# A gated convolution and neighbourhood-attention block: first norm weights as a row, conv tiles read three at a time, four reorderings in the queues

## What is computed

```python
h = rmsnorm(x, norm_g); proj = h @ w_in            # 1024 -> 9 x 1024
a_val, a_glu, z_a, q, k, v, z_b, g_logits = split(proj)
u   = a_val * sigmoid(a_glu)
c   = depthwise_conv31(u) + dw_b
y_a = (silu(layernorm(c, ln_g, ln_b)) * silu(z_a)) @ w_pw_a
attn = neighbourhood_attention(q, k, v, rpb)       # 16 heads, windows of 8 rows x 16 columns
y_b = (attn * silu(z_b)) @ w_o_b
merged = sigmoid(g_a) * y_a + sigmoid(g_b) * y_b   # gates from g_logits + b_gate
y = rmsnorm(x + merged @ w_out, final_g)
```

## Time and profile before

| | |
|---|---|
| median of 3 runs | 1765.33 us |
| the profiled execution, its own time | 1764.42 us |
| its span (first to last instruction) | 1762.5 us |
| PE, DVE, ACT, POOL busy | 1733.1, 1172.5, 468.3, 207.0 us |
| share of PE in the chain that ended last | 92% |
| mean granted TensorE clock | 0.996 |

### The profile page before, as it was taken

How to read it: one execution, slowest core, us unless ns; L and a number is a source line. 1 busy time by engine, 2 the same in 40 slices (tenths; PEclk the granted TensorE clock), 3 DMA queues, 4 the chain that set the end, 5 groups by cost and what they waited for, 6 DMA issues and landing times.

```text
span 1762.5 us, 24610 instructions
## 1 busy us (share of the span) xinstructions
PE 1733.1 (98%) x8652; PEld 1411.5 (80%) x8652; DVE 1172.5 (67%) x1765; ACT 468.3 (27%) x925; POOL 207.0 (12%) x250
## 2 busy tenths in 40 slices
PE   7999999999999999999999999999999899999998
PEld 6888877888888888888887888888777778887886
DVE  4439255897688589579768948957975677335332
ACT  5421123123122122222312212222224234102222
POOL 1120011011011011101101101110200063000001
PEclk9999999999999999999999999999999899999999
DMA  7151335545436525534543562553567565543223
GB/s 289 56 106 48 99 99 143 159 122 160 123 90 170 159 61 156 149 95 133 155 126 85 169 166 54 145 168 90 141 200 291 175 192 179 191 133 105 73 84 132
DMA packets 293893, 240.97 MB, mean 137 GB/s; under 512 B 117222, under 2 KB 248310, under 8 KB 293658
## 3 DMA queue, kind: packets, MB, share of 16 engines
q1 hardware_dynamic: 241482, 145.69, 30.3%
q10 hardware_dynamic: 48432, 79.97, 13.3%
q0 software_dynamic: 3872, 13.75, 3.0%
HBM read 155.10 MB, written 84.23 MB: 136 GB/s over the span
## 4 chain that ended last, share of the span: by engine, by line
PE 92%; DVE 3%; DMA 3%; ACT 1%; issue 1%; ACTq 0%; SPq 0%; DVEq 0%
PE pg L1436 69%; PE pg L1454 15%; PE pO L1546 4%; PE pS L1529 3%; DVE work L1325 2%; DMA qk<-gb_d 1%; DMA work<-tb_d 1%; DVE xs L1065 1%; DMA work<-p_d 1%; ACT xs L828 0%; DMA raw<-in_w_in 0%; DVE ws L1057 0%; PE pS L1470 0%; DVE work L1346 0%; PE pO L1470 0%
## 5 line engine op out<-in xcount | busy, mean ns | idle before, releaser
L1436 PE MATMUL pg<-xs,ws 128*128 128x512 f32 x5688 | 1317.7, 392 | 8.9 <-DVE work L1346 6.6
L1436 PEld LDWEIGHTS pg<-xs,ws 128*128 128x128 f32 x5688 | 1064.7, 188 | 244.7 <-issue 15.2
L1141 DVE SCALAR_TENSOR_TENSOR work<-work 128x1551 f32<-128x1551 f32 x240 | 438.4, 1827 | 4.6
L1454 PE MATMUL pg<-ws,xs 128*128 128x512 f32 x1008 | 238.7, 393 | 3.3 <-DVE ws L1057 2.2
L1454 PEld LDWEIGHTS pg<-ws,xs 128*128 128x128 f32 x1008 | 189.8, 189 | 44.0 <-DVE ws L1057 4.1
L646 POOL TENSOR_TENSOR work<-work 128x384 f32<-128x384 bf16 (+1 forms) x72 | 62.7, 870 | 984.2 <-DVE small L1213 973.7
L1213 DVE CUSTOM_DVE_ANT_0 work<-pS,work 128x384 f32<-128x384 f32 (+1 forms) x192 | 88.4, 511 | 114.9 <-PE pS L1529 114.8
L916 ACT ACTIVATE work<-work,small 128x384 f32<-128x384 f32 (+1 forms) x192 | 109.2, 570 | 158.4 <-DVE small L1213 158.4
L1057 DVE TENSOR_TENSOR ws<-raw,ws 128x1024 fp32r<-128x1024 f32 x89 | 109.7, 1234 | 48.5 <-ACT ws L697 48.4
L697 ACT ACTIVATE ws<-raw 128x1024 fp32r<-128x1024 f32 x89 | 93.5, 1053 | 119.4 <-PE pg L1436 98.7
L1225 DVE STREAM_TRANSPOSE work<-work 128x384 f32<-128x384 f32 (+1 forms) x192 | 102.6, 534 | 6.6
(11 more groups left out here) (98 smaller groups left out, 928.4 us busy)
## 6 DMA issues: line engine op xcount, KB each, us to landing
raw<-in_w_in SPq DMA_DIRECT2D x70, 512.0 KB, 4.5
p_d<-work SPq DMA_DIRECT2D x256, 96.0 KB, 2.2
work<-p_d ACTq DMA_DIRECT2D x64, 384.0 KB, 4.5
work<-v_d SPq DMA_DIRECT2D x128, 96.0 KB, 2.7
p_d<-work SPq DMA_DIRECT2D x128, 64.0 KB, 1.9
work<-p_d ACTq DMA_DIRECT2D x32, 256.0 KB, 4.4
v_d<-work ACTq DMA_DIRECT2D x24, 256.0 KB, 2.0
za_d<-work ACTq DMA_DIRECT2D x24, 256.0 KB, 2.1
```

What stands on the lines that cost most here:

```text
L1141: nc.vector.scalar_tensor_tensor(cv[:, 0:CLEN], u[:, k:k + CLEN], cur[:, k:k + 1], cv[:, 0:CLEN], ALU.mult, ALU.add).then_inc(tap_ok, 1)
L1436: last = nc.tensor.matmul(pg[b][:], wt(s, wpart)[:, k * P:(k + 1) * P], xs[:, k, xpart, chunk(n)], start=(k == 0 and wpart == 1), stop=(k ...
L1454: last = nc.tensor.matmul(pg[b][:], xs[:, k, xpart, t * P:(t + 1) * P], wt(s0 + k // 2, wpart)[:, chunk(k % 2)], start=(k == 0 and xpart = ...
```

## The change

There are five parts. (1) `norm_g` is also loaded as one row of 4 KB, by a transfer issued from ACT's queue; PE multiplies a row of 128 ones with it (two matmuls with a contraction of 1) so that it stands in two PSUM banks on all partitions, and four transposes of the identity run ahead of them. `normalise(0)` reads these banks, in two halves, each with its own count, and PE transposes half by half. The 512 KB load to all partitions stays for the other token tiles and moves behind weight pieces 0 and 1 and token tile 1. (2) In the last unit the two early `tb_d` loads move behind the stores of blocks 10 and 11. (3) In SP's loop of phases 1 and 2 the gate tile is loaded ahead of the weight piece. (4) From the fourth on, conv tile k is loaded once the mean has been taken off tile k-3. (5) On DVE, piece S_OUT+3 is split after two of the eight subtractions of `refill_lo(3, 1)` and `gate(47)`; the other six follow it.

```diff
--- before.py
+++ after.py
@@ -213,6 +213,8 @@
         ngb = work[:, 9 * D:10 * D]
         raw2 = work[:, 11520:11520 + 2 * D].rearrange("p (s d) -> p s d", s=2)
         msk32 = work[:, 11520:11520 + MASKLEN]
+        grow = work[0:1, 15680:15680 + D]
+        onerow = work[0:1, 16704:16704 + P]
         prow = work[:, 14656:14656 + D]
         table = work[:, 0:RROWS * RCOLS]
 
@@ -300,7 +302,7 @@
         x_hi, x_lo = sem("x_hi"), sem("x_lo")
         w_ld = [sem(f"w_ld{i}") for i in range(2)]
         w_ld2 = [sem(f"w_ld2{i}") for i in range(2)]
-        ng_in = sem("ng_in")
+        ng_in, gr_in, ng_ps = sem("ng_in"), sem("gr_in"), sem("ng_ps")
         w_hi, w_lo = sem("w_hi"), sem("w_lo")
         w_used = sem("w_used")
         g_done = sem("g_done")
@@ -428,10 +430,10 @@
                 sp.dma_start(xt[:, t % 8, :], tok_rows(x_prompt, x_sample, t)).then_inc(x_in[t % 8], 16)
 
             load_x(0)
-            sp.dma_start(ngb, norm_g[0:1, :].to_broadcast([P, D])).then_inc(ng_in, 16)
             for s in range(2):
                 piece_s(s, w_rows(w0, C_V * P, s))
             load_x(1)
+            sp.dma_start(ngb, norm_g[0:1, :].to_broadcast([P, D])).then_inc(ng_in, 16)
             for s in range(2, 4):
                 piece_s(s, w_rows(w0, C_V * P, s))
             for t in range(2, 8):
@@ -524,11 +526,11 @@
                         piece(s, w_tile(w0, i * P + ahead[n] * P), 8 * i + (s - 1))
                     elif last and n == 4:
                         piece_y(S_YB)
-                    if last and n == 5:
-                        load_tb_early()
                     if n < BLOCKS // 2:
                         store_probs(i, 2 * n)
                         store_probs(i, 2 * n + 1)
+                    if last and n == 5:
+                        load_tb_early()
                     if n == 4 and not last:
                         load_rel(i + 1, 18 * i + 18)
                     if n == len(ahead) - 2 and n >= 6 or n == 5 and len(ahead) == 6:
@@ -568,13 +570,13 @@
                 sp.wait_ge(st_out[n], 128 + 48 * PAIRS)
             for e in range(2 * 24):
                 ct, n = (e % 24) // NCH, e % NCH
-                if n == 0:
-                    piece_y(S_YB + e // NCH + 3)
                 if e >= 3:
 
                     b, _, out = grs(G_YB + e - 3)
                     sp.wait_ge(g_out[b], out)
                     load_gate(e)
+                if n == 0:
+                    piece_y(S_YB + e // NCH + 3)
                 if e == 24:
 
                     sp.wait_ge(ta_ok, 3 * KT)
@@ -613,7 +615,8 @@
         def _(pool):
             nc.gpsimd.memset(ident[:], 0.0).then_inc(const_ok, 1)
             nc.gpsimd.memset(half, -0.5).then_inc(const_ok, 1)
-            pool.wait_ge(const_ok, 2)
+            nc.gpsimd.memset(onerow, 1.0).then_inc(const_ok, 1)
+            pool.wait_ge(const_ok, 3)
             nc.gpsimd.affine_select(out=ident[:], in_=ident[:], compare_op=ALU.not_equal, fill=1.0, base=0,
                                     pattern=[[-1, P]], channel_multiplier=1).then_inc(const_ok, 1)
             for t in range(NT):
@@ -657,6 +660,8 @@
             for k in range(KT):
 
                 pool.wait_ge(x_lo, 5 * KT + k + 1 if k < KT - 2 else 6 * KT)
+                if k >= 3:
+                    pool.wait_ge(dev, k - 2)
                 pool.dma_start(cs[:, k, :], c_d[k]).then_inc(c_in[k], 16)
 
             pool.wait_ge(var_ok, 1)
@@ -750,6 +755,7 @@
                 act.dma_start(v_d[t * P:(t + 1) * P, chunk(c)], stage[:, g % 3, :]).then_inc(st_out[g % 3], 16)
 
 
+            act.dma_start(grow, norm_g[0:1, :]).then_inc(gr_in, 16)
             square(0)
             split_s(0)
             h_hi(0, 0)
@@ -1074,9 +1080,15 @@
 
             def normalise(t):
 
+                dve.wait_ge(rstd_ok, t + 1)
                 if t == 0:
+                    for hf in range(2):
+                        dve.wait_ge(ng_ps, hf + 1)
+                        x = xt[:, 0, chunk(hf)]
+                        nc.vector.scalar_tensor_tensor(x, x, rstd[:, 0:1], pS[hf][:], ALU.mult, ALU.mult).then_inc(xn_ok, 1)
+                    return
+                if t == 1:
                     dve.wait_ge(ng_in, 16)
-                dve.wait_ge(rstd_ok, t + 1)
                 x = xt[:, t % 8, :]
                 nc.vector.scalar_tensor_tensor(x, x, rstd[:, t:t + 1], ngb, ALU.mult, ALU.mult).then_inc(xn_ok, 1)
 
@@ -1365,10 +1377,12 @@
                     if tile == KT - 1 and n >= 1:
                         if n == 1 and phase == 3:
                             split_s(S_OUT + 2)
-                        refill_lo(phase, n - 1, lambda k: cs[:, k, chunk(n - 1)], 0.5)
+                        ks = range(2) if n == 2 and phase == 3 else range(KT)
+                        refill_lo(phase, n - 1, lambda k: cs[:, k, chunk(n - 1)], 0.5, ks)
                 gate(e0 + 23)
                 if phase == 3:
                     split_s(S_OUT + 3)
+                    refill_lo(phase, 1, lambda k: cs[:, k, chunk(1)], 0.5, range(2, KT))
                 else:
                     refill_lo(phase, 2, lambda k: cs[:, k, chunk(2)], 0.5)
 
@@ -1461,8 +1475,8 @@
 
             def h_t(t):
 
-                pe.wait_ge(xn_ok, t + 1)
                 for hf in range(2):
+                    pe.wait_ge(xn_ok, t + 2 if t else hf + 1)
                     if 2 * t + hf >= 4:
 
                         pe.wait_ge(x_lo, 2 * t + hf - 3)
@@ -1479,7 +1493,12 @@
                                                ident[0:NPAR, 0:NPAR])
                 last.then_inc(par_ps, 1)
 
-            pe.wait_ge(const_ok, 3)
+            pe.wait_ge(const_ok, 4)
+            for k in range(4):
+                nc.tensor.transpose(pg[1][:, k * P:(k + 1) * P], ident[:], ident[:])
+            pe.wait_ge(gr_in, 16)
+            for hf in range(2):
+                nc.tensor.matmul(pS[hf][:], onerow, grow[:, chunk(hf)], start=True, stop=True).then_inc(ng_ps, 1)
             h_t(0)
             for t in range(NT):
                 token_group(t, 0, t, 0, True, t + 1 if t + 1 < NT else None)
```

## The result

The changed kernel takes 1749.22 us in the median of 4 runs (1746.58 to 1750.26), the kernel before 1765.14 beside it; the ratio is 0.9912, 95% interval 0.9900 to 0.9924. On a second chip it was 1749.17 against 1764.15, ratio 0.9918 (0.9902 to 0.9935). That is 15 to 16 us where 11.5 were forecast, and the time lies 2 us under the range. The profiled execution has a span of 1744.8 us against 1762.5.

What follows compares the result with a forecast made beforehand. PE was taken as the bound, busy 1733.1 of 1762.5 us, leaving about 30 us to win. Gains of 0.7 + 1.8 + 6.8 + 2.2 = 11.5 us gave a median of 1753.8 us, range 1751.3 to 1758.3.

Steps and rivals of the forecast that it cites:

- the stretch from 190 to 1190 us: Middle of the kernel: PE waits for nothing to speak of, so what the start gains isn't eaten there.
- the sum: Whole kernel: gains of 0.7 + 1.8 + 6.8 + 2.2 = 11.5 us.
- part 2: Early tb loads behind the stores: PE's waits for probabilities near 1310 us shrink, 1.8 us faster.
- Parts 3 and 4: Attention branch's output: the 4.51 us gate wait goes whole, plus 2.3 us of lower clock, together 6.8 us.
- Part 1's own chain: Kernel start: PE begins at about 9.6 us, then waits for weight piece 2, second transposes about 14.9; gain 0.7 us.
- The two products: Kernel start: two added fp32 128x512 matmuls take 1.7 us each, 3.4 in all, within PE's 7.8 idle us.
- The lower clock level at the start: Kernel start: matmul spacing is 0.42 us each against 0.23 later; a possible earlier clock rise was counted as nothing.
- the next pair of loads: Next probability loads, issued about 1314.4 and needed at 1319.6, may meet the tb loads: 0.2 us charged, bound 2.
- the clock: Behind the 4.51 us gate wait: PE's clock fell to 1.2 GHz; avoiding that gives 2.3 us.
- Part 5: Entry of the output projection: PE's 2.23 us wait for piece S_OUT+3 goes, 2.2 us, bounds 1.9 and 2.3.
- The LayerNorm's scaling: From 1431 to 1463 us: PE waits 1.5 us in three pieces; the stretch moves forward as a block, unchanged.
- the four terms: The gains summed: start 0.7 us, early reloads 1.8, gate and conv tiles 6.8, fourth split 2.2.

Runs made afterwards that it cites:

- Part 1 alone: Kernel before with only the norm-weight row, later 512 KB load, halves and four transposes added: 1760.55 us against 1764.04, ratio 0.9982.
- the 28 idle instructions in the kernel before: Kernel before with fourteen transposes of the identity at the head of PE's list, nothing else: 1761.78 us against 1764.73, ratio 0.9987.
- part 1 undone with and without them: Changed kernel with the norm-weight edit taken back: 1749.69 us with fourteen idle transposes at PE's head, 1751.83 us without.
- the second profile of the kernel before: The unchanged kernel run once more with a profile: 1766.74 us (one run), span 1764.8.
- the filler: Kernel before with 16 idle instructions (four identity transposes, two small products) at the head of PE's list: 1777.60 us against 1764.15, ratio 1.0077.

## Why the prediction was wrong, step by step

- **What failed: the stretch from 190 to 1190 us.** The prediction says there that PE "waits for nothing to speak of" and takes it as fixed. The list of waits had a row of 2.3 us at issue, five times, 0.6 at the longest, which I passed over because nothing in the change touches the loop. It was 2.8 us of cost, PE waiting in each turn for instructions that had to be fetched anew, and part 1 took it away by moving PE's code on (26 instructions by the spot: 18 and the four transposes' 8). Part 1 alone, the 28 idle instructions in the kernel before, and part 1 undone with and without them show it. Of the 3.5 us by which the change gave more than the sum (15.0 on the second chip against 11.5), this is the greater part. The sign of the effect was luck: 8 instructions fewer and the change would have brought nothing.
- **What stays open.** The change gave 0.7 to 1.6 us more than the sum with these 2.8, though part 2 fell short by 1.0. Parts 3 and 4 cover some of it (7.6 for 6.8); the rest is open. One thing that the sum left out could lie in it: a short wait can cost more than its length. In the second profile of the kernel before, the granted clock was 0.50 for 3 us behind the 1.63 us wait on probabilities (1312.9 to 1315.9) and behind the 2.23 us wait on the split (1630 to 1633); in the first it was 1.00 in both places.
- **Part 1's own chain was right.** PE at 9.6 (9.58), waiting then for piece 2, transposes at 14.9 (14.72); the start gives 0.6 to 0.9 us in two profiles of the changed kernel (0.4 in that of part 1 alone), forecast 0.7. The two products took 3.78 us, forecast 3.4; the first needed bank was ready in time. The load of the row landed by 2.75 to 3.2 us. The lower clock level at the start was read from the spacing of the matmuls. The profiles of before and after print a granted clock of 1.00 there, but their first record of it comes only later; the one profile with an earlier record, that of the 28 idle instructions, shows 0.50 from 9 to 15 us, with the same 12 matmuls in 5.02 us, and so bears the reading out.
- **Part 2: the right mechanism, the wrong size.** Forecast 1.8 us, with 0.2 charged for the next pair of loads. The new wait is 1.3 to 1.8 us, not 0.2, so most of the 2.0 us came back on the spot; alone the part measured 0.8 us. The failed term is the landing of the second pair: I had allowed 5.2 us from issue to need, and the two loads landed 6.0 and 7.0 us after issue in the first profile, 6.6 and 7.5 in the second.
- **Parts 3 and 4: right, and the clock with them.** Forecast 6.8. By the two traces the distance from the group after the 0.64 us wait to the end of group 9 shrank by 7.1 us (1354.52 to 1405.40 against 1349.14 to 1392.96); the medians give 7.6 for both parts, 6.7 and 7.1 for each alone. The gate tiles land 6.5 to 7.9 us after issue, within the 9 named, and the granted clock is 1.00 from 1340 to 1390. That each part does it alone I had left open.
- **Part 5: right**, 2.2 us.
- **The LayerNorm's scaling: too firm.** I wrote that this stretch "neither grows nor shrinks". It lost PE 1.5 us of waits before, none in the first profile after, 1.4 in the second, 1.0, 1.3 and 1.9 in three variants. The same kernel gave 0 and 1.4, so the difference belongs to the execution and not to the change; it accounts for a part of the 17.7 us between the two profiled spans, and for none that can be told in the medians.
- The range reached 2.5 us to the fast side for known terms only. A term of unknown sign for moved code would have belonged in it, on both sides, and by these runs as wide as 3 us down and 13 up. Its arithmetic was loose too: the bounds of the four terms, added up, give 1752.7 to 1756.6, not the "own range" of 1752.2 to 1755.2.

## What to carry to other kernels

Any instruction added ahead of a loop on an engine moves the loop's body in the instruction stream, and where PE has little work between the head and the first instructions that must be fetched anew, each turn can pay for it: compare the time of a turn and the packets on the instruction queue within the loop's stretch (here none against nine a turn) before crediting an edit with a gain, and try some idle instructions at the head before anything cleverer. When one small load is late behind large ones, changing its place in its own queue and limiting the large ones are two cures for one illness; one is enough. A reload moved out of the way of one deadline meets the next one: check the landing of whatever follows it.

## What the runs showed of the hardware

**A turn of the loop** costs PE 0, 0.5 or 3.1 to 3.3 us according to the place of the code alone, with no change to the work, and 16 idle instructions made a kernel of 1764 us 13.5 us slower. The packet of instructions that PE waits for starts 0.1 to 0.6 us after the head, and PE goes on 2.2 to 2.8 us after that.

**The same short wait takes the clock down in some turns and not in others.** Behind the filler's five waits of 1.9 to 2.1 us the granted clock fell to 0.50 three times (1.4 to 1.6 us more each) and stayed at 1.00 twice.

**The clock also fell with PE never idle.** Ahead of group 10 PE does 24 matmuls of one column in 2.7 us. Towards their end the granted clock falls in most kernels and stays at the lower level of 1.2 GHz for some 3.4 us. The window behind them, in the second run of the changed kernel and in the one with parts 3 and 4 (columns as in the earlier trace rows):

```profile
1395.90:1399.30 3.40, 3.40 (x10) 2.63 (x10) 1.98 (x2) 1.13 (x2) 2.30 (x1) 0.51 0.30 113
```

```profile
1402.00:1405.50 3.50, 3.50 (x18) 2.90 (x18) 1.97 (x2) 1.13 (x2) 2.30 (x1) 1.00 0.31 116
```

The distance from these matmuls to the next column sum is 9.8 us in one case and 8.1 in the other. Of 16 profiled executions 11 had the long one, the kernel before and the changed one among them. Kernels with the same list on PE had either, so the list alone doesn't settle it, and that the one-column matmuls are the cause isn't shown; whether one kernel has both in different executions wasn't seen. It is 1.6 us, and nothing was tried against it.
